# Reordering the first block of a seven-product fp32 layer: first splits, second step, squares, turns, and the order of the block's products

## What is computed

```
hn   = rmsnorm(x, norm_w)
proj = hn @ w_in                      # 2048 -> q, k, v, g_attn, h, c_gate, b_gate, g_conv
attn = sliding-window attention(q, k, v, sinks, rel_bias)      # chunks of 64, own and previous
conv = b_gate * causal_depthwise_conv3(c_gate * h)
mixed = concat(attn * silu(g_attn), conv * silu(g_conv))
out  = rmsnorm(x + mixed @ w_out, final_norm_w)
```

## Time and profile before

| | |
|---|---|
| median of 3 runs | 1350.67 us (1349.51 to 1350.72) |
| profiled execution | 1351.28 us, its span 1349.5 us |
| TensorE busy | 1329.4 us (99% of the span) |
| VectorE, ScalarE, GpSimd busy | 918.9 (68%), 539.3 (40%), 91.0 (7%) |
| mean granted TensorE clock | 0.997 |
| DMA | 390 MB, mean 289 GB/s |

### The profile page before, as it was taken

The page is one execution under the profiler, slowest core; times in us unless marked ns, Lnnn a source line. Parts: engine busy times, 40 slices in busy tenths (PEclk is TensorE's granted clock), DMA queues, the critical chain, the costliest instruction groups (busy, mean ns, idle before and its releaser), DMA issues.

```text
span 1349.5 us, 16546 instructions
## 1 busy us (share of the span) xinstructions
PE 1329.4 (99%) x6022; PEld 1098.9 (81%) x6022; DVE 918.9 (68%) x1142; ACT 539.3 (40%) x939; POOL 91.0 (7%) x153
## 2 busy tenths in 40 slices
PE   9999999999999999999999999999999999999997
PEld 7778888888878888888888888878888888888886
DVE  5898876324477458984589855998439896665376
ACT  7754532322232433434334343343423444321454
POOL 1222311000000000000000000000000221100001
PEclk9999999999999999999999999999999999999999
DMA  9778995998878999879998799987998888899768
GB/s 364 282 274 290 405 377 173 304 308 309 314 252 247 285 292 292 246 220 312 296 291 250 225 290 288 288 256 236 300 330 300 319 274 274 288 313 356 279 253 308
DMA packets 205056, 390.02 MB, mean 289 GB/s; under 512 B 78992, under 2 KB 128176, under 8 KB 183344
## 3 DMA queue, kind: packets, MB, share of 16 engines
q1 hardware_dynamic: 185376, 321.83, 72.9%
q0 software_dynamic: 18304, 62.92, 12.7%
q10 hardware_dynamic: 1296, 4.22, 0.8%
HBM read 294.18 MB, written 98.93 MB: 291 GB/s over the span
## 4 chain that ended last, share of the span: by engine, by line
PE 88%; DVE 5%; issue 3%; DMA 2%; ACT 1%; SPq 1%; POOL 0%; DVEq 0%; ACTq 0%; POOLq 0%
PE banks L1962 84%; PE banks L1985 1%; PE banks L1997 1%; DMA qkv_park<-e 1%; DMA raw<-in_w_in_dram 1%; DVE w_ring L1336 1%; PE banks L2006 1%; PE banks L2007 1%; DVE raw L1426 1%; DMA x_far<-x_park 0%; DVE e L1515 0%; DVE z L1398 0%; DVE x_main L1349 0%; DVE raw L1432 0%; ACT z L1207 0%
## 5 line engine op out<-in xcount | busy, mean ns | idle before, releaser
L1962 PE MATMUL banks<-x_main,w_ring 128*128 128x512 f32 x2352 | 551.7, 392 | 4.2 <-DVE x_main L1349 2.5
L1962 PEld LDWEIGHTS banks<-x_main,w_ring 128*128 128x128 f32 x2352 | 438.9, 188 | 95.6 <-issue 5.5
L976 ACT ACTIVATE w_ring<-raw 128x1024 fp32r<-128x1024 f32 x223 | 235.5, 1056 | 555.1 <-PE banks L1962 542.9
L1336 DVE TENSOR_TENSOR w_ring<-raw,w_ring 128x1024 fp32r<-128x1024 f32 x223 | 273.0, 1224 | 217.9 <-ACT w_ring L976 217.7
L1962 PE MATMUL banks<-x_far,w_ring 128*128 128x512 f32 x1680 | 393.4, 391 | 2.0 <-DMA x_far<-x_park 1.9
L1962 PEld LDWEIGHTS banks<-x_far,w_ring 128*128 128x128 f32 x1680 | 313.0, 188 | 66.7 <-issue 2.1
L1962 PE MATMUL banks<-w_ring,x_main 128*128 128x512 f32 x1008 | 230.6, 389 | 0.8 <-DVE x_main L1349 0.8
L1962 PEld LDWEIGHTS banks<-w_ring,x_main 128*128 128x128 f32 x1008 | 189.1, 188 | 40.6 <-issue 1.2
L499 POOL DMA_DIRECT2D x_park<-x_main x104 | 56.1, 540 | 1016.8 <-DVE x_main L1349 1016.8
L1007 ACT ACTIVATE x_main<-z 128x512 fp32r<-128x512 f32 x104 | 64.9, 624 | 129.2 <-issue 102.3
L1349 DVE TENSOR_TENSOR x_main<-z,x_main 128x512 fp32r<-128x512 f32 x104 | 71.5, 687 | 41.0 <-ACT x_main L1007 41.0
(11 more groups left out here) (153 smaller groups left out, 858.2 us busy)
## 6 DMA issues: line engine op xcount, KB each, us to landing
x_far<-x_park SPq DMA_DIRECT2D x84, 1024.0 KB, 7.5
x_main<-x_park SPq DMA_DIRECT2D x84, 1024.0 KB, 7.3
x_park<-x_main POOLq DMA_DIRECT2D x104, 512.0 KB, 5.6
raw<-in_w_in_dram SPq DMA_DIRECT2D x130, 256.0 KB, 5.9
raw<-in_w_out_dram SPq DMA_DIRECT2D x32, 512.0 KB, 6.1
raw<-in_w_in_dram SPq DMA_DIRECT2D x31, 512.0 KB, 11.8
q_cur<-qkv_park SPq DMA_DIRECT2D x64, 128.0 KB, 5.8
z<-mix_park SPq DMA_DIRECT2D x16, 512.0 KB, 7.8
```

Source lines behind the costliest of these rows:

```text
L976: act.activation(w_ring[:, n % NW, :, 0, :], raw[:, c, k:k + 2, :], ACT.Copy).then_inc(w_hi_ready, 1)
L1336: dve.tensor_tensor(w_ring[:, n % NW, :, 1, :], raw[:, c, k:k + 2, :], w_ring[:, n % NW, :, 0, :], ALU.subtract).then_inc(w_lo_ready, 1)
L1962: op = pe.matmul(bank, left, right, start=(first and i == 0), stop=(kt == HK - 1 and i == 2), skip_group_check=goes_on)
```

## The change

The first block's order becomes 2, 1, 5, 3, 6, 7, 4 and product 3 goes on in the banks of 5 there too, which makes 5 a copied product (16 sums on VectorE where 20 were, 12 copies on ScalarE where 8 were). The other parts: the first splits are x before w; the load of the second step's weights goes ahead of its x, step 2's weights ahead of its last x; step 1 is written out by parts, so that it begins with the high parts alone; step 2's splits go ahead of three of the squares; VectorE makes the last of the eight squares; two turns and the sum over partitions go later; one turned tile uses bank 3. The core of the diff (w_count(n) is n + 2, a new count for the same semaphore):

```
-ORDER = [(2, 1, 3, 6, 7, 5, 4)] + ...
+ORDER = [(2, 1, 5, 3, 6, 7, 4)] + ...
-COPIED = [(o[0], 3, 7) if b in ON_CHIP else ...
+COPIED = [(2, 5, 3, 7) if b == GATES else (o[0], 3, 7) if b == OUT0 else ...
-ADDED = [(o[1], 6, 5, 4) if b in ON_CHIP else ...
+ADDED = [(1, 6, 7, 4) if b == GATES else (o[1], 6, 5, 4) if b == OUT0 else ...
-            if p == 3 and b not in ON_CHIP:
+            if p == 3 and b != OUT0:
                 goes_on = 5
-BANK0 = (4, 5, 6, 7, 6, 7, 6, 7)
+BANK0 = (4, 5, 6, 7, 6, 7, 6, 3)
-TURN0_AT = {(2, 1): (0,), (2, 2): (1,), (2, 3): (2,), ...
+TURN0_AT = {(2, 3): (0,), (3, 0): (1,), (3, 2): (2,), ...
-SQUARE_HI_AT = {(0, 1): 0, (0, 2): 1, (0, 3): 2, (1, 0): 3}
-SQUARE_LO_AT = {(1, 1): (0,), (1, 2): (1,), (2, 1): (2,), (2, 2): (3,)}
-ADD_SQUARES_AT = {(0, 2): (0,), (1, 2): (1, 2, 3)}
-SUM_AT = (2, 2)
-VAR0_AT = (2, 3)
+SQUARE_HI_AT = {(0, 1): 0, (0, 3): 1, (1, 0): 2, (1, 1): 3}
+SQUARE_LO_AT = {(1, 2): (0,), (2, 0): (1,), (2, 1): (2,)}
+SQUARED_BY_DVE = (2, 1)
+ADD_SQUARES_AT = {(1, 0): (0,), (1, 3): (1, 2, 3)}
+SUM_AT = (3, 0)
+VAR0_AT = (2, 2)
-W_HI_AT = {(1, 0): 2, ...      (W_LO_AT the same)
+W_HI_AT = {(0, 2): 2, ...
-S1_AT = {(5, 0): 0, (7, 0): 1, (7, 2): 2, (8, 0): 3}
-S24_AT = {(6, 1): 0, (7, 1): 1, (7, 3): 2, (8, 2): 3}
+S1_AT = {(5, 0): 0, (7, 0): 1, (7, 2): 2, (9, 0): 3}
+S24_AT = {(9, 2): 0, (10, 2): 1, (11, 2): 2, (12, 2): 3}
-X_HI_AT = {(1, 0): (4, 5), (2, 0): (6, 7), ...      (X_LO_AT the same)
+X_HI_AT = {(0, 2): (4, 5), (1, 1): (6, 7), ...
-        park_stage = [e[:, i, 2 * j:2 * j + 2, :] for i in (1, 3) for j in range(2)]
+        park_stage = [e[:, 3, 2 * j:2 * j + 2, :] for _ in range(2) for j in range(2)]
             load_first(HK + 1)
+            load_raw(GATES, 0, 5)
             load_xt(5)
-            load_raw(GATES, 0, 5)
             load_xt(6)
+            load_raw(GATES, 0, 6)
             load_xt(7)
             load_x_low(0)
-            load_raw(GATES, 0, 6)
-                        if i == 4 and q >= 2 and quarter in (0, 2):
+                        if i == 5 and q >= 2 and quarter in (0, 2):
                             load_more(q - 2, quarter // 2)
-                        elif p == 5:
+                        elif p == (6 if b == GATES else 5):
                             load_raw(b + 1, 1, q)
-                p = (ORDER[GATES][1], 5, 5, 4)[i]                     # tanh_gate
+                p = (1, 7, 6, 4)[i]
-                        if (i, q) == (4, 1) and quarter in (1, 3):
+                        if (i, q) == (4, 3) and quarter in (1, 3):
                             tanh_gate(0, quarter // 2)
-            w_hi_first(0)                                             # ScalarE; VectorE alike
             x_hi(0, 0)
+            w_hi_first(0)
+            x_hi(0, 1)
             w_hi_first(1)
-            x_hi(0, 1)
-                        if quarter == 1 and 12 <= n < 12 + QP:
-                            s3(GATES, n - 12)
+                        if quarter == 1 and 16 <= n < 16 + QP:
+                            s3(GATES, n - 16)
-                        late = 1 if b == GATES else 0                 # t2, from step 7 + late
+                        late = 4 if b == GATES else 0
-                        late = 2 if b == GATES else 0                 # t3, from step 10 + late
+                        late = 6 if b == GATES else 0
-                        if (i, q) == (4, 2) and quarter in (1, 3):
+                        if (i, q) == (5, 0) and quarter in (1, 3):
                             silu_gate(0, quarter // 2)
-                if b == GATES and p == 3:                             # wait_bank
+                if b == GATES and p == 5:
+            def second_step():
+                for i in range(2):
+                    pe.wait_ge(w_hi_ready, w_count(1))
+                    pe.wait_ge(x_hi_ready, 3 + i)
+                    for t in range(4):
+                        product(GATES, 2, 2 + i, t, 1, (0,))
+                    pe.wait_ge(w_lo_ready, w_count(1))
+                    for t in range(4):
+                        product(GATES, 2, 2 + i, t, 1, (2,))
+                    pe.wait_ge(x_lo_ready, 3 + i)
+                    for t in range(4):
+                        op = product(GATES, 2, 2 + i, t, 1, (1,))
+                op.then_inc(step_done, 1)
```

More of the change, by code:

```diff
@@ L68 @@
 TAIL = 3
-COPIED = [(o[0], 3, 7) if b in ON_CHIP else (o[0], 6, 7) for b, o in enumerate(ORDER)]
-ADDED = [(o[1], 6, 5, 4) if b in ON_CHIP else (o[1], 5, 3, 4) for b, o in enumerate(ORDER)]
+COPIED = [(2, 5, 3, 7) if b == GATES else (o[0], 3, 7) if b == OUT0 else (o[0], 6, 7) for b, o in enumerate(ORDER)]
+ADDED = [(1, 6, 7, 4) if b == GATES else (o[1], 6, 5, 4) if b == OUT0 else (o[1], 5, 3, 4) for b, o in enumerate(ORDER)]
 QKV_KEYS = (True, False, True, False)
@@ L93, in copy_count @@
 def copy_count(b, p, t):
-    return sum(3 * w for w in WIDE[:b]) + COPIED[b].index(p) * WIDE[b] + t + 1
+    return sum(len(c) * w for c, w in zip(COPIED[:b], WIDE)) + COPIED[b].index(p) * WIDE[b] + t + 1
 def sum_count(b, p, t):
@@ L142, in _banks @@
             loose = []
-            if not (p in (1, 6) or (p == 5 and b not in ON_CHIP)):
+            if not (p in (1, 6) or (p == 5 and b != OUT0)):
                 loose = mine
@@ L485, in conv_count, with w_count @@
             return 20 * (b - CONV0) + i
+        def w_count(n):
+            return n + 2
         def mix_count(i):
@@ L511, in load_raw @@
                     p = {(0, 0): 7, (0, 1): 3, (1, 0): 5, (1, 1): 4}[c, j // QP]
-                    sp.wait_ge(w_lo_ready, at(b - 1, p, j % QP) + 1)
+                    sp.wait_ge(w_lo_ready, w_count(at(b - 1, p, j % QP)))
+                    if b == QKV and (c, j // QP) == (1, 0):
+                        sp.wait_ge(s2_ready, j + 1)
                 if b == GATES:
@@ L1009, in w_hi_first @@
             def w_hi_first(i):
-                act.wait_ge(raw_loaded[4] if i else first_loaded, 16 if i else 48)
-                act.activation(w_ring[:, 0, i, 0, :], raw[:, 0, HK + i, :], ACT.Copy).then_inc(w_hi_ready if i else w_first_hi, 1)
+                act.wait_ge(raw_loaded[4] if i else w_first_loaded, 16)
+                act.activation(w_ring[:, 0, i, 0, :], raw[:, 0, HK + i, :], ACT.Copy).then_inc(w_hi_ready, 1)
             def square_hi(i):
@@ L1216, in _ @@
             act.activation(table_dump, minus_half, ACT.Copy)
+            act.wait_ge(first_loaded, 32)
+            x_hi(0, 0)
             w_hi_first(0)
-            x_hi(0, 0)
+            x_hi(0, 1)
             w_hi_first(1)
-            x_hi(0, 1)
             w_hi(1)
@@ L1497, in sums @@
                     dve.tensor_tensor(e2, e2, ps, ALU.add).then_inc(sum_ready, 1)
-                elif p == 5 and b in ON_CHIP:
+                elif p == 7:
+                    dve.wait_ge(copy_ready, copy_count(b, 7, t))
+                    dve.tensor_tensor(e1, e1, e3, ALU.add).then_inc(sum_ready, 1)
+                elif p == 5 and b == OUT0:
                     dve.wait_ge(copy_ready, copy_count(b, 7, t))
@@ L1511, in sums @@
                 else:
-                    dve.wait_ge(sum_ready, sum_count(b, 5, t))
+                    dve.wait_ge(sum_ready, sum_count(b, 7 if b == GATES else 5, t))
                     if b == OUT1:
@@ L1951, in product @@
                 w, a = w_ring[:, n % NW, kt % 2, :, :], x_halves(n)[kt % 2]
-                goes_on = p in (6, 7) or (p == 3 and b not in ON_CHIP)
+                goes_on = p in (6, 7) or (p == 3 and b != OUT0)
                 first = kt == 0 and not goes_on
@@ L2037, in _ @@
                 product(GATES, 2, 0, t, 0, (0,))
-            pe.wait_ge(w_first_lo, 1)
-            for t in range(4):
-                product(GATES, 2, 0, t, 0, (2,))
             pe.wait_ge(x_lo_ready, 1)
@@ L2043, in _ @@
                 product(GATES, 2, 0, t, 0, (1,))
+            pe.wait_ge(w_lo_ready, 1)
+            for t in range(4):
+                product(GATES, 2, 0, t, 0, (2,))
+            def second_step():
[8 more added lines that the diff above has]
+                    pe.wait_ge(x_lo_ready, 3 + i)
+                    for t in range(4):
+                        op = product(GATES, 2, 2 + i, t, 1, (1,))
+                op.then_inc(step_done, 1)
             for n in range(STEPS - TAIL):
                 b, p, q = place(n)
+                if n == 1:
+                    second_step()
+                    continue
                 for t in range(WIDE[b]):
```

88 lines of the change are left out of this document (51 added, 37 removed).

## The result

The changed kernel takes 1359.55 us (median, 1357.27 to 1360.74) beside 1350.7 for the kernel before: ratio 1.006, 95% interval 1.0049 to 1.0071. It is slower by 8.9 us. Medians and ratios are of undisturbed executions; one of gaps_closed, at 2883.86 us, is left out.

A forecast was written before the change was run, and what follows sets the result against it. PE was busy 1329.4 of 1349.5 us, so only its gaps and clock could move the time. Terms -1.3 - 4.1 + 1.6 + 3.1 + 3.7 = +3.0, plus 0.9 for slow clock, gave 1354.6 us; 8-in-10 range 1345.5 to 1358.

The forecast's parts named there:

- The loads into QKV: Steps 28 and 29: later loads leave DMA idle earlier, so step 29's x lands near 191.3 us; +3.7 us.
- the 0.9 us for the slow clock: After the waits of steps 20 and 28: PE's lower granted clock costs 0.9 us for both together.
- Head: First steps: the gap before step 1 goes (-1.5), the factors come slightly late (+0.2); -1.3 us, between -2.5 and 0.
- Step 8: Before step 8: the last placements end earlier, so the 2.5 us gap and 1.6 us of slow clock go; -4.1 us.
- VectorE: +1.6 and +3.1: VectorE's fuller queue makes PE wait at steps 13 and 14 (+1.6 us) and at three tiles of step 20 (+3.1 us).
- Sum at step 28: Terms ahead of the QKV loads: head -1.3, step 8 -4.1, VectorE's queue +1.6 and +3.1; together -0.7 us.
- A: Rival: VectorE is late but the loads are in time; -0.7 us, about 1350.0 us; chance 0.15.
- B: Rival: the loads are late but VectorE's work fits; -1.7 us, 1349.0 us; chance 0.13.
- C: Rival: neither VectorE nor the loads are late; -5.4 us or a bit more, 1345.3 us, faster; chance 0.16.
- D: Rival: step 8's bank wait stays, placements as late as before; +7.1 us, 1357.8 us or less; chance 0.08.
- the 4.9 in full: Upper bound for the QKV loads, +5 us: all 4.9 us of DMA time idle in steps 18 to 20.

The follow-up runs named there:

- gaps_closed: head_only with weight tile 9's high half made in step 8, weight differences later and three low halves of weights moved on VectorE in steps 2 to 5: 1352.61 us.
- more_late_alone: The kernel before with only the four 512 KB transfers of extra QKV weights issued at steps 22 and 23 instead of 18 and 19, in 512-byte pieces: 1353.18 us.
- more_late_wide: The kernel before with the same four transfers at steps 22 and 23, in 4 KB pieces of other weights (K and V weights wrong): 1353.64 us.
- head_only: The kernel before with the first six steps reordered alone, the first block's products in the old order: 1348.93 us, ratio 0.9984.
- wide_pieces: The whole change with the four late weight transfers in 4 KB instead of 512-byte pieces, same bytes of other weights (K and V weights wrong): 1354.72 us.

## Why the prediction failed
**Place and sign were right, the size of one term was not.** The failed step is "The loads into QKV", +3.7 us, with the 0.9 us for the slow clock. Measured, the two are 11.1 us where 4.6 stood: step 28 began 188.59 - 180.49 = 8.1 us after PE could have begun it (180.78 less the 0.29 explained below), and its matmuls took 3.0 us more at the low clock. The 1.4 us that come back later stood in no term.

**Head: -1.3.** Measured up to step 8: step 13 starts at 94.99 after 0.87 us of gap, and a gap counts 0.29 more than its bracket (the last matmuls end after the next could begin: 1.36 us for six at full pace, 1.65 in the rows of step 20). So without waits it were 93.83, and step 8 five steps of 5.44 earlier, 66.63, against 67.72 - 0.29 = 67.43: -0.8. The gap before step 1 went. Two things took part of it back. The first product began at 7.25 against 6.53, which is no work of the change: it begins at 6.55 and 7.40 in more_late_alone and more_late_wide, which are alike up to there, and at 6.01 to 7.50 with the new head. Without it the head is worth -1.5. And the wait for the factors is 1.2 us for 0.3. GpSimd's power took 1.86 us for 1.04, beside a low half of w that VectorE now makes at that moment (gaps_closed, without it there, has 0.4 us again):

```profile
26.37 1.86 POOL L922 TENSOR_TENSOR small<-small 128x4 f32<-128x4 f32 x1 [24.91 <-DVE small L1403]
```

**Step 8: -4.1.** Right: no gap, clock 1.00. By starts it was worth 70.23 - 67.43 = 2.8, and 180.80 - 70.23 - 20 x 5.44 = 1.8 of slow clock: -4.6. That the slow clock is in the profile of the kernel before is in part luck: head_only has the same gap and a clock of 1.00 behind it.

**VectorE: +1.6 and +3.1.** Right. By starts, steps 13 and 14 lose 100.93 - 93.83 - 5.44 = 1.7, and step 20 loses 3.4: tile 1 would have begun at 100.93 + 34.00 = 134.93 and tile 3 at 137.65, and begins at 141.03. The brackets show 1.1 and 2.5. The clock didn't fall there.

**Sum at step 28:** -0.8 - 4.6 + 1.7 + 3.4 = -0.3, where I had -0.7.

**Loads: +3.7.** The bytes that don't pass in time were well sized: 4.9 us by the forecast, 4.4 by the windows. (Steps 18 to 20 alone: 223 GB/s in 19.7 us against 379 in 16.3, also 1.8 MB less. The DMA share there is 0.64, not 0.75, as PE's waits stretch these steps.) With 4 KB pieces step 29's x lands at 191.2, 16.1 us after its issue at 175.08, where the forecast said "near 191.3". That it agrees so closely is partly luck: this execution began its first product 0.5 us earlier than the kernel before, and it stopped before steps 27 and 28 (1.16 and 2.65 us) for VectorE, not for x. Two things were missing. The four transfers come in 512-byte pieces, and I counted them as bytes; beside a full store queue they got 10.0% of the engines for 6 us, while SyncE, whose program holds x of step 28 behind them, stood in their issue. Their length makes the 4.8 us between 1354.72 and 1359.55. And the slow clock: I took 0.9 us for both stretches; step 28 alone lost 8.44 - 5.44 = 3.0, after a wait of 7.8 us and not of 3.3, and step 20 lost none.

I had this in hand and set it aside. The Trainium skill (DMA: Bandwidth & Descriptors, section Queues, rings and completion order) says that an engine goes from queue to queue packet by packet. I read it as an even split of time and held the uneven row against it, but there a packet of the stores has 3.6 KB on average and one of the loads 1.6 KB; the row couldn't speak for 512 bytes alone. Turns by packet give a queue of short pieces few bytes, and the traces agree: 323 and 313 packets in 6 us for 512 bytes and 1 KB, and from 160 to 166 us one packet for one, 598 of loads and 599 of stores in the change, 414 and 417 in wide_pieces. From 154 to 160 us alone the store queue has about twice as many in the change and in the two kernels with longer pieces; why is open.

**The rivals.** A, B and C needed loads or VectorE in time; neither was. D fell: step 8's wait went. No rival had the loads later than their bytes, and none had `xw`, the second path to step 28, in it. The range ended at 1358 because its upper bound for the loads was +5, "the 4.9 in full", a bound on bytes alone.

**What stays open.** Why the pieces' length costs x of step 28 so much more in the whole change than in more_late_alone is argued from the issue times and the queues, not shown. How the 4.8 us split between bytes not moved, the order of the loads and the slow clock is open too.

## What to carry to other kernels
When a transfer is moved, look at the length of its pieces and at what is in the other queues there, and not only at its bytes: beside a full queue of wide pieces, short ones got a share by number here, and everything later in the issuing engine's program waited with them. Bound such a term by the time of a held-up issue, not by bytes. A named releaser that ends just before PE starts is to be checked against the landing of the transfer that the step needs. And when two variants wait equally long, look at what each waits for before calling the cause the same.

## What the runs showed of the hardware
- An engine that issues a transfer can stand in the issue for over 11 us, with transfers of short pieces ahead in its queue: 11.41 on SyncE, and 13.27 on ScalarE, whose work stood 11.48. From GpSimd the four transfers of `load_more` took 0.9 us each to issue.
- The same gap of 2.51 us before step 8 brought the low clock in two profiles and not in two others. From 70 to 72 us it was 0.59 in more_late_alone and 1.00 in more_late_wide, which have the same program up to there; the earlier trace rows has 0.58, head_only 1.00. So part of the 4.6 us at step 8 belongs to some executions only. After a wait of 2.65 us (wide_pieces, step 28) it stayed full, 5.7 us for 24 matmuls. After the five longer ones at steps 27 and 28 it was low each time: 24 matmuls took 7.8 (after 4.55), 7.9 (5.68), 7.7 (6.16), 8.2 (7.43) and 8.6 us (7.81), where 5.6 is full pace.
- A GpSimd operation on 128x4 took 1.04 us alone and 1.86 beside a VectorE operation of 128x1024. In the kernel before one of 128x1024 on VectorE took 3.44 us beside one of the same size on GpSimd (2.91 us, from 172.79), and 1.21 without.
